# Activation parts side by side in one 512-column product: output phases and heads of a two-block sequence model

## What is computed

```python
def _layer_ab(x, ...):                      # 8 dilated heads, 4 difference heads
    h = _rmsnorm_2(x, norm_g) @ w_in        # q, k, v, z of each head
    ya = _dilated_mixture(rope(aq), rope(ak), av)
    yb = (softmax(q1 k1^T) - lam * softmax(q2 k2^T)) v      # causal
    yb = _rmsnorm_2(yb, subln_g) * (1.0 - lam_init)
    return x + (concat(ya, yb) * silu(z)) @ w_out
def _layer_c(x, ...):                       # 16 causal heads, same form
    return x + (causal_attention(rope(cq), rope(ck), cv) * silu(z)) @ w_out
```

## Time and profile before

| | us |
|---|---|
| three runs | 2569.82, 2574.58, 2577.92 |
| median | 2574.58 |
| the profiled execution | 2571.68 |
| its span, first to last instruction | 2569.9 |

### The profile page before, as it was taken

One profiled execution on the slowest core, in us unless ns is written; L12 is line 12 of the kernel. 1 busy time (PEld: TensorE's weight loads), 2 busy tenths in 40 slices (PEclk: granted clock), 3 DMA queues, 4 the chain that ended last, 5 costly groups with the idle time before them and its releaser, 6 DMA issues.

```text
span 2569.9 us, 65229 instructions
## 1 busy us (share of the span) xinstructions
PE 2452.5 (95%) x26124; PEld 2192.2 (85%) x26124; DVE 1345.2 (52%) x2114; ACT 1162.0 (45%) x1712; POOL 1371.5 (53%) x570
## 2 busy tenths in 40 slices
PE   6798999999999799998999999999999999999997
PEld 2277777777777578878999999999999999999997
DVE  5948787778777333335655545444444443343322
ACT  6643443444334234344444455444455554444453
POOL 0032221222122044345888887777778878777775
PEclk9899999999999799999999999999999999999999
DMA  9831211111111022224776754455445544455553
GB/s 354 276 112 52 67 46 48 61 59 46 53 54 51 12 91 79 92 82 154 259 256 236 245 187 162 165 171 172 164 155 166 185 165 165 169 172 165 170 173 131
DMA packets 100144, 361.40 MB, mean 141 GB/s; under 512 B 11120, under 2 KB 14320, under 8 KB 99728
## 3 DMA queue, kind: packets, MB, share of 16 engines
q1 hardware_dynamic: 99072, 357.96, 41.1%
q10 hardware_dynamic: 912, 1.03, 0.1%
HBM read 356.85 MB, written 2.10 MB: 140 GB/s over the span
## 4 chain that ended last, share of the span: by engine, by line
PE 86%; issue 6%; DVE 4%; ACT 2%; DMA 1%; POOL 1%; DVEq 0%; SPq 0%; ACTq 0%; POOLq 0%
PE ps L183 17%; PE ps L184 17%; PE ps L185 17%; PE ps L578 5%; PE ps L580 4%; PE ps L579 4%; PE ps L664 2%; PE ps L730 2%; PE ps L750 1%; PE ps L799 1%; PE ps L767 1%; PE ps L309 1%; DVE wlo L408 1%; PE ps L649 1%; DMA W<-stream 1%
## 5 line engine op out<-in xcount | busy, mean ns | idle before, releaser
L171 POOL TENSOR_TENSOR wlo<-raw,whi 128x1024 fp32r<-128x1024 f32 x563 | 1370.3, 2446 | 1176.5 <-ACT whi L161 1040.0
L183 PE MATMUL ps<-ahi,whi 128*128 128x256 f32 (+1 forms) x3712 | 1087.9, 293 | 16.7 <-POOL wlo L171 6.5
L184 PE MATMUL ps<-alo,whi 128*128 128x256 f32 (+1 forms) x3712 | 1073.3, 289 | 0.0
L185 PE MATMUL ps<-ahi,wlo 128*128 128x256 f32 (+1 forms) x3712 | 1073.0, 289 | 0.0
L161 ACT ACTIVATE whi<-raw 128x1024 fp32r<-128x1024 f32 x566 | 595.1, 1056 | 450.9 <-PE ps L185 376.1
L183 PEld LDWEIGHTS ps<-ahi,whi 128*128 128x128 f32 x3712 | 713.5, 192 | 30.6 <-issue 13.1
L184 PEld LDWEIGHTS ps<-alo,whi 128*128 128x128 f32 x3712 | 713.6, 192 | 8.8
L185 PEld LDWEIGHTS ps<-ahi,wlo 128*128 128x128 f32 x3712 | 713.0, 192 | 8.0
L578 PE MATMUL ps<-ahi,whi 128*128 128x256 f32 (+1 forms) x512 | 199.5, 390 | 2.9 <-ACT W L929 2.9
L580 PE MATMUL ps<-ahi,wlo 128*128 128x256 f32 (+1 forms) x512 | 173.6, 339 | 1.1 <-issue 1.1
L579 PE MATMUL ps<-alo,whi 128*128 128x256 f32 (+1 forms) x512 | 173.7, 339 | 0.0
(11 more groups left out here) (339 smaller groups left out, 3274.0 us busy)
## 6 DMA issues: line engine op xcount, KB each, us to landing
raw<-stream SPq DMA_DIRECT2D x566, 512.0 KB, 3.3
W<-stream SPq DMA_DIRECT2D x64, 512.0 KB, 5.1
graw<-stream SPq DMA_DIRECT2D x32, 512.0 KB, 4.3
W<-xT SPq DMA_DIRECT2D x1, 4096.0 KB, 17.6
XR<-xT SPq DMA_DIRECT2D x16, 128.0 KB, 5.0
outT<-XR SPq DMA_DIRECT2D x4, 512.0 KB, 3.0
cns<-consts SPq DMA_DIRECT2D x1, 1120.0 KB, 5.3
cns<-consts SPq DMA_DIRECT2D x1, 896.0 KB, 8.7
```

Source lines behind the costliest of these rows:

```text
L171: nc.gpsimd.tensor_tensor(wlo[slot], raw[slot], whi[slot].bitcast(F32), ALU.subtract).then_inc(lo_done, 1)
L183: nc.tensor.matmul(out, whi[slot][:, k, :], mh, start=first and k == 0, stop=False)
L184: nc.tensor.matmul(out, whi[slot][:, k, :], ml, start=False, stop=False)
L185: ins = nc.tensor.matmul(out, wlo[slot][:, k, :], mh, start=False, stop=last and k == UK - 1)
```

## The change

In the output phases and all heads of the second block, high and low activation parts lie side by side in one tensor (`acts`, `mhl`). `mm_wide` multiplies the high weights with both at once, 512 columns into a whole bank of PSUM, and the low weights with the high part, 256 columns into the bank's first half. A k-tile has two matmuls in place of three. The bank's halves must now be added: in the output phases by a second VectorE step on the residual, in the heads by a copy of the second half on ScalarE (`parts_copy`) and a sum on VectorE (`parts_sum`). Query and key are turned tile by tile, from the summed half into the other half of the same bank. The tiles take other banks. In the difference head the value's scaling moves ahead of the softmax mix on VectorE, and the transposes of the mix move behind the first unit of the last tile on TensorE. The stages before `out1` keep `mm_unit`.

```diff
-        ahi = sb("ahi", 2 * KT * T, F32R).ap().rearrange("p (s k t) -> p s k t", s=2, k=KT)
-        alo = sb("alo", 2 * KT * T, F32R).ap().rearrange("p (s k t) -> p s k t", s=2, k=KT)
+        acts = sb("acts", 4 * KT * T, F32R).ap().rearrange("p (b s k t) -> p b s k t", b=2, s=2, k=KT)
+        ahi, alo = acts[:, 0], acts[:, 1]
...
+        def parts_copy(act, held, bank):
+
+            return nc.scalar.activation(held, ps[:, bank, T:], ACT.Copy)
+
+        def parts_sum(dve, held, bank):
+
+            return nc.vector.tensor_tensor(ps[:, bank, 0:T], ps[:, bank, 0:T], held, ALU.add)
+
+        def mm_wide(pe, slot, s, bank, hl, k0, first, last, tile_ready=None):
+
+
+            pe.wait_ge(lo_done, s + 1)
+            both_parts = ps[:, bank, :].rearrange("p (b t) -> p b t", b=2)
             ins = None
...
                     tile_ready(k0 + k)
-                mh, ml = (ahi[:, sel, k0 + k, :], alo[:, sel, k0 + k, :]) if hi_ is None else \
-                    (hi_[:, k0 + k, :], lo_[:, k0 + k, :])
-                nc.tensor.matmul(out, whi[slot][:, k, :], mh, start=first and k == 0, stop=False)
-                nc.tensor.matmul(out, whi[slot][:, k, :], ml, start=False, stop=False)
-                ins = nc.tensor.matmul(out, wlo[slot][:, k, :], mh, start=False, stop=last and k == UK - 1)
+                nc.tensor.matmul(both_parts, whi[slot][:, k, :], hl[:, :, k0 + k, :], start=first and k == 0, stop=False)
+                ins = nc.tensor.matmul(ps[:, bank, 0:T], wlo[slot][:, k, :], hl[:, 0, k0 + k, :], start=False,
+                                       stop=last and k == UK - 1)
             return ins.then_inc(unit_used, 1)
...
-                            nc.vector.scalar_tensor_tensor(x, ps[:, bank + n, 0:T], g, x, ALU.mult, ALU.add).then_inc(done.sem, 1)
+                            nc.vector.scalar_tensor_tensor(x, ps[:, bank + n, 0:T], g, x, ALU.mult, ALU.add)\
+                                .then_inc(N["half"].sem, 1)
+                            N["half"].wait(dve, i * 2 + n + 1)
+                            nc.vector.scalar_tensor_tensor(x, ps[:, bank + n, T:], g, x, ALU.mult, ALU.add).then_inc(done.sem, 1)
...
-                    hi(3)
-                    act.wait_ge(unit_used, i * U_HEAD + (base + 4))
-                    A["t2"].wait(act, i)
-                    for h in range(2):
-                        nc.scalar.activation(rot[64 * h:64 * h + 64, :], ps[64 - 64 * h:128 - 64 * h, 0, :], ACT.Copy)\
-                            .then_inc(A["rot"].sem, 1)
-                    hi(4, 5, 6)
+                    for b in range(2):
+                        act.wait_ge(unit_used, i * U_HEAD + (base + 2 * b + 2))
+                        A["qk"].wait(act, 2 * i)
+                        parts_copy(act, rot[:, T * b:T * b + T], b).then_inc(A["copy"].sem, 1)
+                        A["part"].wait(act, 4 * i + b + 1)
+                        for h in range(2):
+                            nc.scalar.activation(ps[64 * h:64 * h + 64, b, T:], ps[64 - 64 * h:128 - 64 * h, b, 0:T], ACT.Copy)\
+                                .then_inc(A["rot"].sem, 1)
...
+                        if b == 0:
+                            hi(3)
+                    hi(4, 5)
+                    act.wait_ge(unit_used, i * U_HEAD + (base + 6))
+                    parts_copy(act, vf, 2).then_inc(A["copy"].sem, 1)
+                    hi(6)
                     for k in range(2):
...
                     hi(7)
+                    act.wait_ge(unit_used, i * U_HEAD + (base + 8))
+                    parts_copy(act, zz, 7).then_inc(A["copy"].sem, 1)
                     A["vt_mm"].wait(act, i + 1)
...
-                    A["rot"].wait(dve, 2 * i + 2)
                     A["done"].wait(dve, i)
-                    nc.vector.tensor_tensor(rot, rot, sn, ALU.mult).then_inc(A["t2"].sem, 1)
-                    nc.vector.tensor_tensor(qk, ps[:, 0, :], cs, ALU.mult).then_inc(A["t1"].sem, 1)
-                    A["t1"].wait(dve, i + 1)
-                    A["t2"].wait(dve, i + 1)
-                    nc.vector.tensor_tensor(qk, qk, rot, ALU.add).then_inc(A["qk"].sem, 1)
-                    dve.wait_ge(unit_used, i * U_HEAD + (base + 6))
-                    nc.vector.tensor_tensor(vf, ps[:, 1, 0:T], scale, ALU.mult).then_inc(A["vf"].sem, 1)
+                    for b in range(2):
+                        half = slice(T * b, T * b + T)
+                        A["copy"].wait(dve, 4 * i + b + 1)
+                        parts_sum(dve, rot[:, half], b).then_inc(A["part"].sem, 1)
+                        A["rot"].wait(dve, 4 * i + 2 * b + 2)
+                        nc.vector.tensor_tensor(rot[:, half], ps[:, b, T:], sn[:, half], ALU.mult).then_inc(A["t2"].sem, 1)
+                        nc.vector.tensor_tensor(ps[:, b, 0:T], ps[:, b, 0:T], cs[:, half], ALU.mult).then_inc(A["t1"].sem, 1)
+                        A["t1"].wait(dve, 2 * i + b + 1)
+                        A["t2"].wait(dve, 2 * i + b + 1)
...
-                    tile(2, ps[:, 0, T:])
-                    tile(4, ps[:, 1, 0:T])
-                    tile(6, ps[:, 1, T:])
-                    tile(8, ps[:, 2, 0:T])
-                    B["qk"].wait(pe, 2 * i + 2)
+                    def tile(k):
+                        mm_wide_tile(pe, base, i, U_DIFF, k, k // 2 % 4, acts[:, :, 0])
+
+                    def wide(k, k0):
+                        mm_wide(pe, (base + k) % RING, i * U_DIFF + (base + k), 3, acts[:, :, 0], k0, k0 == 0, k0 > 0)
+                    tile(2)
+                    B["zs"].wait(pe, i)
+                    tile(4)
+                    tile(6)
+                    B["qk"].wait(pe, 4 * i + 1)
+                    tile(8)
+                    B["qk"].wait(pe, 4 * i + 4)
                     for b in range(2):
...
-                    tile(10, ps[:, 2, T:])
-                    tile(12, ps[:, 3, 0:T])
+                    tile(10)
+                    tile(12)
...
+                    wide(14, 0)
...
-                    tile(14, ps[:, 3, T:])
+                    wide(15, UK)
...
-                    def turned(b):
-                        act.wait_ge(unit_used, i * U_DIFF + (base + 4 + 4 * b))
+                    def turned(n):
+                        act.wait_ge(unit_used, i * U_DIFF + (base + 2 * n + 2))
+                        B["qk"].wait(act, 4 * i)
+                        parts_copy(act, rot2[:, n // 2, n % 2 * T:n % 2 * T + T], n).then_inc(B["copy"].sem, 1)
+                        B["part"].wait(act, 8 * i + n + 1)
                         for h in range(2):
-                            nc.scalar.activation(rot2[64 * h:64 * h + 64, b], ps[64 - 64 * h:128 - 64 * h, b, :], ACT.Copy)\
+                            nc.scalar.activation(ps[64 * h:64 * h + 64, n, T:], ps[64 - 64 * h:128 - 64 * h, n, 0:T], ACT.Copy)\
                                 .then_inc(B["rot"].sem, 1)
...
+                    turned(0)
                     hi(3)
-                    B["t2"].wait(act, 2 * i)
-                    turned(0)
-                    hi(4, 5, 6, 7)
                     turned(1)
-                    hi(8, 9, 10)
+                    hi(4, 5)
+                    turned(2)
...
+                    hi(6, 7)
+                    turned(3)
+                    hi(8, 9)
+                    copied(vf2, 4)
+                    hi(10)
                     exps(0)
                     hi(11)
                     exps(1)
+                    copied(vf2, 5)
...
+                    copied(zz2, 7)
...
+                    for m in range(2):
+                        B["copy"].wait(dve, 8 * i + m + 5)
+                        parts_sum(dve, vf2[:, m * T:m * T + T], m).then_inc(B["part"].sem, 1)
+                    B["part"].wait(dve, 8 * i + 6)
+                    nc.vector.tensor_tensor(halves2(vf2), ps[:, 0:2, 0:T], s2, ALU.mult).then_inc(B["vf"].sem, 1)
...
-                    dve.wait_ge(unit_used, i * U_DIFF + (base + 12))
-                    nc.vector.tensor_tensor(halves2(vf2), halves2(ps[:, 2, :]), s2, ALU.mult).then_inc(B["vf"].sem, 1)
-                    dve.wait_ge(unit_used, i * U_DIFF + (base + 16))
-                    nc.vector.tensor_tensor(halves2(zz2), halves2(ps[:, 3, :]), s2, ALU.mult).then_inc(B["zs"].sem, 1)
+                    for m in range(2):
+                        B["copy"].wait(dve, 8 * i + m + 7)
+                        parts_sum(dve, zz2[:, m * T:m * T + T], 2 + m).then_inc(B["part"].sem, 1)
+                    B["part"].wait(dve, 8 * i + 8)
+                    nc.vector.tensor_tensor(halves2(zz2), ps[:, 2:4, 0:T], s2, ALU.mult).then_inc(B["zs"].sem, 1)
```

112 lines of the change are left out of this document (68 added, 44 removed).

## The result

The changed kernel takes 2546.1 us (median of four runs, 2544.5 to 2550.65) against 2573.64 (2569.82 to 2577.92), a ratio of 0.9895 (95% interval 0.9875 to 0.9916). The profiled execution took 2545.25 us (span 2543.5), 26.4 less than that of before, where the sum said 33.0.

The account below looks back on a forecast made before the run. TensorE's matmul starts bound the kernel. -36.9 - 2.4 + 0.8 + 1.0 + 2.8 + 1.7 = -33.0 us gives 2538.7 from the profiled 2571.68, 2541.6 from the median; forecast 2540, range 2532 to 2549, 2554 with the last rival.

Parts of the forecast that it names:

- signs: Expected in the trace: starts 0.227 and 0.120 us apart, causal head 24.1, difference head 2.5 shorter without score wait, clock 1.00.
- Products: Output phases and heads: a unit takes 2.775 us instead of 2.880, over 352 units; gain 36.9 us.
- Scores: Difference heads: the score matmul's idle time behind the rotary chain's last step goes; gain 2.4 us. Plain heads: nothing.
- Evictions of the first output phase: Two VectorE steps instead of one delay the bank's release; 0 to 0.55 us in each of 7 passes, 2.8 taken.
- Gates: Last dilated and last causal head: ScalarE copies the gate before the transposed values, +0.4 us each, 0.8 in all.
- End of the difference heads: Gate scaling, tanh and square chain on ScalarE: +0.8 us for copy and sum, 0.2 for shorter units; 1.0.
- Seams and end: Mean matmul waits for the last running sum: +0.8 us after first output phase, +0.4 after second, +0.5 at program end; 1.7.
- The slower rival: 24 plain heads: turned copies of about 2.4 us each instead of 0.35 make the score matmul wait; 3%.
- The late mix: Difference heads: value scaling gains two copies and sums (1.6 us) and loses the two mix steps ahead of it.

Follow-up runs that it names:

- the fusion undone: Against the changed kernel, each k-tile is three 256-column matmuls again, with evictions, rotary chain, banks and late mix kept; 2575.25 us, 1.0008 of before.
- four banks: Against the changed kernel, the first output phase's passes take four PSUM banks in turn instead of two; 2543.75 us, 0.9888 of before.
- the second trace: The changed kernel traced once more with nothing altered; 2540.7 us span.
- Eight and eight: Against the changed kernel, each unit runs its eight 512-column matmuls first, then the eight 256-column ones; 2549.3 us, 0.9902 of before.
- two and two: Against the changed kernel, each unit runs wide, wide, narrow, narrow, four times, instead of in turn; 2543.8 us in one run.
- mix early: Against the changed kernel, difference heads' mix steps go back ahead of the value sums, mix transposes ahead of the unit between; 2559.06 us, 0.9946 of before.

## Why the prediction was right, and where not

The sign and the place were right, the time 6 us low: 2540 against 2546.1, inside the range. Three of the signs came: 0.227 and 0.120 us between starts on the fast rate, no wait at the scores of the difference heads, the clock at 1.00 up to the last product. Two came smaller: a causal head takes 24.20 us and not 24.1, a difference head is 2.2 us shorter and not 2.5. Point by point:

- **Products** (-36.9): the term that was mis-sized. The k-tile distances of the changed kernel put it at 31.0. "I take each at its own distance", from streams of one width, held for about two k-tiles in three; in the heads a stream that mixes the widths is 23 ns a unit dearer. 5.9 us short.
- **Scores** (-2.4): the difference heads gave it (51.19 to 50.30 with the fusion undone, no wait after). But "it has no slack and costs nothing in a plain head" was wrong: the first score matmul of the earlier trace rows stood 0.32 us ahead of the next kind (2205.62, 2205.94), now 0.22, and 24 heads gave 0.09 more each, 2.2 us that I did not count. In all 24 plain heads of the kernel before, the step ended 0.07 us before that start: the matmul was waiting for it, though the profile names no wait. The sum for the new chain was off as well: its parts add to 3.4 us and not 3.1, and the trace has 2.9. With 5.5 of cover that changes nothing.
- **Evictions of the first output phase** (+2.8): the starts of its seven later passes show 0.65 us above the plain distance in the first and 0.25 to 0.4 in the others, 2.7 in all. Right, and with four banks it was gone.
- **Gates** (+0.8): 1.4 us in two waits against 1.3, so 0.1. The transposes, not the copy of the gate, come last there. **End of the difference heads** (+1.0): 1.5 and 1.2 against 0.7 and 1.0, right. **Seams and end** (+1.7): 7.3 against 6.6, so 0.7.
- **Not in the sum**: 1.0 us at the transposes of the first dilated head, a normalising step held by GpSimd (absent in the second trace); 0.5 at the end, where the last mean matmul ran at a clock of 0.50 behind a wait of 2.5; and the 2.3 us of chance ahead of the change.

These make -31.0 - 2.4 - 2.2 + 2.7 + 0.1 + 1.0 + 0.7 + 1.0 + 0.5 + 2.3 = -27.3, against -26.4 measured; 0.9 is not accounted for. In part the errors cancel: the 2.2 us that I did not count and the 1.7 that gates and seams cost less stand against 3.8 us that were not in the sum. The products alone missed by nearly as much as the whole.

- **The slower rival.** Its chance of 3% came out of a wrong price. I let it begin at a chain of 7.3 us, 1.7 past the cover. Measured: 1.5 us more of copies (a pair is 0.74), well inside the cover, make the kernel 75 us slower, 45 in waits and much of the rest in the clock behind them. The turned copies cost 0.37 each as taken, so the case did not arise; had the key tile's pair cost 1.5 more, the change would have been a loss. I had seen steps "until a GpSimd instruction ended" and concluded that those with one input in PSUM run free. That is right, and the new sums do. I did not ask which old steps run between SBUF and SBUF beside GpSimd, and what the moved high parts would do to them.
- **The late mix** I priced as a small swap for the value scaling. It is worth about 10 us in the difference heads: without it the changed order of ScalarE and VectorE puts the mix steps, 2.77 us for two in the same head before the change, on two whole low parts in two heads of four.

## What to carry to other kernels

Price a merged matmul from a stream with the same mix of shapes; where there is none, leave room for less (here a sixth of the gain, a fifth in the heads, did not come). Cover that TensorE leaves is not all the cover there is: when a step on ScalarE grows or moves, lay GpSimd's new times over VectorE's steps from SBUF to SBUF, and let such a step read PSUM where it can. A wait of 2 us costs almost twice itself when the clock falls behind it. And before a gain of 1 or 2 us is put down to an edit, compare the same stretches of both traces, also those that the edit does not touch.

## What the runs showed of the hardware

- A stream of 512- and 256-column matmuls in turn (fp32r, weights loaded for each) runs at 346.7 or 353.3 ns a pair, constant over a stretch, and can change behind an interruption. The same stretch can have either rate in two traces of one kernel (second output phase, 347.2 and 352.4). Eight and eight or two and two have one rate in between. One width alone: 120.0 and 226.9 ns.
- Two VectorE steps (`tensor_scalar`) of 128x128 and 128x256 fp32 from SBUF to SBUF took 0.81 us with GpSimd's gap beside them, 4.42 under four low parts on end, 0.74 under the same load when they read PSUM.
- A copy of 64x256 from PSUM to PSUM across partitions takes 0.36 us on ScalarE, two on end 0.74.
- Behind waits of 2.59 us (mix early) and 3.44 us (four banks) TensorE's granted clock was 0.50; behind others of 2.7 and 2.8 us, at the seam of the first output phase in the two traces of the changed kernel, it stayed at 1.00. Behind waits of 1.9 us it fell in 14 heads of 24, in one and the same run. The time of the wait alone does not tell.
